# Block attention in four PSUM banks, its steps between the blocks of the first two gate projections; values feature-major

## What is computed

```python
qa, ka, va, qb, kb, vb, ga, gb = split(h @ w_in)      # 8 query heads of 128; ka, va have 2 heads; ga, gb are 2048 wide
ya = global_gqa(rope(rms(qa)), rope(rms(ka)), va)     # full softmax over 256 keys, 8 heads
yb = neighbourhood_attention(qb, kb, vb, nat_rpb)     # softmax over a window, with a bias, 8 heads
merged = sigmoid(ga) * (ya @ w_oa) + sigmoid(gb) * (yb @ w_ob)
x = x + g1 * (merged @ w_out)
# g1 and five more rows of 2048 come from c_act @ w_ada + b_ada
```

## Time and profile before

| | |
|---|---|
| time, median of 3 runs | 2335.82 us (2332.87 to 2339.69) |
| span of the profiled execution | 2332.2 us; its own time is not listed apart, the lowest of the three is 0.7 us above this span |
| PE busy, share of the span | 2252.8 us, 97% |
| DVE, ACT, POOL busy | 1497.0, 1010.8, 242.6 us |
| chain that ended last | PE 78%, DMA 9%, DVE 6%, issue 3%, ACT 2% |
| TensorE clock, mean over the span | 0.981 of full |

### The profile page before, as it was taken

The page is one execution under the profiler, slowest core; times in us unless marked ns, Lnnn a source line. Parts: engine busy times, 40 slices in busy tenths (PEclk is TensorE's granted clock), DMA queues, the critical chain, the costliest instruction groups (busy, mean ns, idle before and its releaser), DMA issues.

```text
span 2332.2 us, 38185 instructions
## 1 busy us (share of the span) xinstructions
PE 2252.8 (97%) x13068; PEld 1982.8 (85%) x13068; DVE 1497.0 (64%) x1990; ACT 1010.8 (43%) x1248; POOL 242.6 (10%) x425
## 2 busy tenths in 40 slices
PE   8999997999999989999999999999999999999997
PEld 6888686988877768899777878879999999998885
DVE  5666577897777857688677777774445444544544
ACT  5444534444444434434644443444434343443432
POOL 1110011212210021101022221210000000000000
PEclk9999998999999997999999999989999999999998
DMA  8786076887885583867359887755555655566563
GB/s 304 250 244 178 22 244 248 254 268 270 304 275 176 174 244 101 263 187 252 109 193 314 311 306 254 262 191 180 181 183 177 189 180 183 179 207 195 187 199 120
DMA packets 196653, 499.07 MB, mean 214 GB/s; under 512 B 29784, under 2 KB 56536, under 8 KB 195648
## 3 DMA queue, kind: packets, MB, share of 16 engines
q1 hardware_dynamic: 163648, 388.03, 51.3%
q0 software_dynamic: 32896, 109.55, 14.1%
HBM read 495.34 MB, written 2.10 MB: 213 GB/s over the span
## 4 chain that ended last, share of the span: by engine, by line
PE 78%; DMA 9%; DVE 6%; issue 3%; ACT 2%; POOL 1%; POOLq 0%; SPq 0%; DVEq 0%; ACTq 0%
PE ps L1678 39%; PE ps L1687 32%; DMA ada_raw<-in_w_ada_dram 6%; PE ps L1747 2%; DVE lo L926 1%; PE ps L1768 1%; PE ps L1838 1%; DVE acc_g L938 1%; DVE acc_s L938 1%; DMA raw<-in_w_in_dram 1%; PE ps L1757 1%; DMA raw<-in_ml_w_in_dram 1%; ACT hi L544 1%; DMA rel<-in_rpbT_dram 1%; DMA xT_raw<-in_xT_dram 0%
## 5 line engine op out<-in xcount | busy, mean ns | idle before, releaser
L926 DVE TENSOR_TENSOR lo<-raw,hi 128x1024 fp32r<-128x1024 f32 x732 | 891.4, 1223 | 631.7 <-ACT hi L544 629.6
L544 ACT CAST hi<-raw 128x1024 fp32r<-128x1024 f32 x732 | 767.8, 1051 | 1144.5 <-PE ps L1678 552.0
L1687 PE MATMUL ps<-XH,hi 128*128 (+1 forms) x1920 | 543.6, 283 | 1.9 <-DVE XL L1042 1.9
L1687 PE MATMUL ps<-XH,lo 128*128 (+1 forms) x1920 | 543.4, 283 | 0.0
L1687 PE MATMUL ps<-XL,hi 128*128 (+1 forms) x1920 | 543.4, 283 | 0.0
L1678 PE MATMUL ps<-hi,XH 128*128 128x512 f32 x1376 | 433.2, 394 | 34.2 <-DVE lo L926 28.4
L1678 PE MATMUL ps<-lo,XH 128*128 128x512 f32 x1376 | 428.9, 391 | 0.0
L1678 PE MATMUL ps<-hi,XL 128*128 128x512 f32 x1376 | 428.0, 390 | 0.0
L1687 PEld LDWEIGHTS ps<-XH,hi 128*128 128x128 f32 x1920 | 368.6, 192 | 2.5 <-DVE XL L1042 2.4
L1687 PEld LDWEIGHTS ps<-XL,hi 128*128 128x128 f32 x1920 | 368.6, 192 | 0.0
L1687 PEld LDWEIGHTS ps<-XH,lo 128*128 128x128 f32 x1920 | 368.6, 192 | 0.0
(11 more groups left out here) (309 smaller groups left out, 1645.6 us busy)
## 6 DMA issues: line engine op xcount, KB each, us to landing
ada_raw<-in_w_ada_dram POOLq DMA_DIRECT2D x384, 256.0 KB, 5.0
raw<-in_w_in_dram SPq DMA_DIRECT2D x136, 512.0 KB, 4.6
raw<-in_ml_w_in_dram SPq DMA_DIRECT2D x128, 512.0 KB, 5.1
raw<-in_w_gate_dram SPq DMA_DIRECT2D x176, 256.0 KB, 2.8
raw<-in_w_up_dram SPq DMA_DIRECT2D x176, 256.0 KB, 3.0
raw<-in_w_down_dram SPq DMA_DIRECT2D x88, 512.0 KB, 4.2
raw<-in_mla_w_in_dram SPq DMA_DIRECT2D x48, 512.0 KB, 5.6
raw<-in_mla_w_out_dram SPq DMA_DIRECT2D x32, 512.0 KB, 4.7
```

The lines of the kernel that those rows point to most:

```text
L544: nc.scalar.copy(hi[:, j, :], raw[:, j, :]).then_inc(hi_ready, 1)
L926: nc.vector.tensor_tensor(lo[:, j, :], raw[:, j, :], hi[:, j, :].bitcast(F32), ALU.subtract) \
L1687: ins = mm(ps[:, o:o + SEQ], w[:, j, m * P:(m + 1) * P], x(k), start=first and lead and m % 2 == 0, stop=last and w is lo, skip_group_chec ...
```

## The change

The block attention no longer stands ahead of the gate projections. It uses banks 4 to 7 only: two for scores, one (`turn_slot`) for the transposed probabilities of a head, one (`value_slot`) for its result. `ga0`, `ga1` and `gb0` all use group 0 (banks 0 to 3). A table `STEPS_AFTER` puts the steps 0 to 35 behind the blocks 0 to 30 counted from the start of `ga0`: one step behind each, two behind blocks 3, 6, 9, 12 and 15. On PE a step stands behind block b; on ACT and DVE the same step stands ahead of `hi` and `lo` of block b+4. Heads of `yb` now come first. DVE scales the probabilities instead of the result. The values are the stationary operand, and the result of a head comes out feature-major (two matmuls 128x256 per head), so the transposes back are gone. ACT copies the transposed probabilities once per head (128x512). The sigmoids of `ga0` and `ga1` are written where `vb_tok`, `kva_tok` and `kaT` lie, so they wait for heads of the attention. `ADA_BESIDE` moves ten ada blocks away from `ga0`.

```diff
-    "ga0@0:act ga1:act gb0:act gb1:act oa0:dve ob0:dve oa1:dve ob1:dve mTa:split4 wo0:dve mTb:split4 wo1@0:dve "
+    "ga0@0:act ga1@0:act gb0@0:act gb1:act oa0:dve ob0:dve oa1:dve ob1:dve mTa:split4 wo0:dve mTb:split4 wo1@0:dve "
...
-              "qa": 16, "kb": 8, "vb": 16, "ga0": 22, "ga1": 22, "gb0": 22, "gb1": 22, "oa0": 6, "ob0": 6, "oa1": 6,
-              "ob1": 6, "wo0": 20, "wo1": 20}
+              "qa": 18, "kva": 4, "kb": 8, "vb": 16, "ga0": 12, "ga1": 22, "gb0": 22, "gb1": 22, "oa0": 6, "ob0": 6,
+              "oa1": 6, "ob1": 6, "wo0": 22, "wo1": 22}
...
+STEPS_AFTER = {}
+_step = 0
+for _block in range(31):
+    _n = 2 if _block in (3, 6, 9, 12, 15) else 1
+    STEPS_AFTER[_block] = tuple(range(_step, _step + _n))
+    _step += _n
...
+        def score_slot(u):
+            return (4 + u % 2) * HALF
+        turn_slot, value_slot = 6 * HALF, 7 * HALF
...
@@ scalar @@
-            attention(A3, 32, prob2, probT2, nmax2, rsum2, lambda u: SEQ,
-                      lambda h: yaH[:, h, :] if h < N_A else ybH[:, h - N_A, :])
+            def blk_step(i):
+                if i < 32:
+                    act.wait_ge(A3["maxed"], i + 1)
+                    if i >= 3:
+                        act.wait_ge(A3["turned"], i - 2)
+                    o = score_slot(i)
+                    nc.scalar.activation(prob2[:, i % 3, :], ps[:, o:o + SEQ], ACT.Exp, bias=nmax2[:, i:i + 1],
+                                         accum_out=rsum2[:, i:i + 1]).then_inc(A3["exped"], 1)
+                if i >= 3 and i % 2 and i < 34:
+                    h = (i - 3) // 2
+                    act.wait_ge(A3["turned"], 2 * h + 2)
+                    if h:
+                        act.wait_ge(A3["summed"], h)
+                    nc.scalar.copy(probT2[:, :, :].rearrange(flat), ps[:, turn_slot:turn_slot + HALF]) \
+                      .then_inc(A3["copied"], 1)
+                if i >= 4 and i % 2 == 0:
+                    h = (i - 4) // 2
+                    H, _, hh = blk_head(h)
+                    act.wait_ge(A3["summed"], h + 1)
+                    nc.scalar.copy(H[:, hh, :], ps[:, value_slot:value_slot + SEQ]).then_inc(A3["hi"], 1)
...
+            for b in range(4, 48):
+                if b == 19:
+                    act.wait_ge(A3["summed"], N_A)
+                    gate("ga0", sig_a, 0)
+                if b == 35:
+                    act.wait_ge(A3["summed"], 2 * N_A)
+                    gate("ga1", sig_a, 1)
+                for i in STEPS_AFTER.get(b - 4, ()):
+                    blk_step(i)
+                hi_block(B_MERGE + b, b % RING, landed(B_MERGE + b, b % RING))
@@ vector @@
+            def blk_step(i):
+                if i < 32:
+                    o = score_slot(i)
+                    dve.wait_ge(A3["scored"], i + 1)
+                    add_bias(i, o)
+                    nc.vector.tensor_reduce(nmax2[:, i:i + 1], ps[:, o:o + SEQ], AX_X, ALU.max, negate=True) \
+                      .then_inc(A3["maxed"], 1)
+                if 1 <= i <= 32:
+                    u = i - 1
+                    dve.wait_ge(A3["exped"], u + 1)
+                    link(nc.vector.reciprocal(rinv2[:, u:u + 1], rsum2[:, u:u + 1]))
+                    nc.vector.tensor_scalar(prob2[:, u % 3, :], prob2[:, u % 3, :], rinv2[:, u:u + 1], None,
+                                            ALU.mult).then_inc(A3["normed"], 1)
+                if i >= 5 and i % 2:
+                    h = (i - 5) // 2
+                    H, L, hh = blk_head(h)
+                    dve.wait_ge(A3["hi"], h + 1)
+                    nc.vector.tensor_tensor(L[:, hh, :], ps[:, value_slot:value_slot + SEQ],
+                                            H[:, hh, :].bitcast(F32), ALU.subtract).then_inc(A3["lo"], 1)
@@ tensor @@
+            def blk_step(i):
+                if i < 32:
+                    h, t = (i % 16) // 2, slice(i % 2 * P, (i % 2 + 1) * P)
...
+                    if i >= 2:
+                        pe.wait_ge(A3["exped"], i - 1)
+                    o = score_slot(i)
+                    mm(ps[:, o:o + SEQ], q, k, start=True, stop=True, skip_group_check=True).then_inc(A3["scored"], 1)
+                if i >= 4 and i % 2 == 0:
+                    h = (i - 4) // 2
+                    pe.wait_ge(A3["copied"], h + 1)
+                    if h >= 1:
+                        pe.wait_ge(A3["lo"], h)
...
+                        ins = mm(ps[:, o:o + SEQ], v, probT2[:, t, :], start=(t == 0), stop=(t == TOK - 1),
+                                 skip_group_check=True)
+                    ins.then_inc(A3["summed"], 1)
+                if 2 <= i < 34:
+                    u = i - 2
+                    pe.wait_ge(A3["normed"], u + 1)
+                    if u >= 2 and u % 2 == 0:
+                        pe.wait_ge(A3["copied"], u // 2)
+                    for t in range(TOK):
+                        o = turn_slot + t * SEQ + u % 2 * P
+                        ins = nc.tensor.transpose(ps[:, o:o + P], prob2[:, u % 3, t * P:(t + 1) * P], ident[:, :])
+                    ins.then_inc(A3["turned"], 1)
...
+            for n, name in enumerate(("ga0", "ga1", "gb0")):
+                token_major(name, B_MERGE + 16 * n, 16, XH, XL, then=blk_after(16 * n))
             pe.wait_ge(A3["lo"], 16)
-            for n, name in enumerate(("ga0", "ga1", "gb0", "gb1")):
-                token_major(name, B_MERGE + 16 * n, 16, XH, XL)
+            token_major("gb1", B_MERGE + 48, 16, XH, XL)
```

More of the change, by code:

```diff
@@ L828, in _ @@
             whole("kaT", kaT[:, :, :].rearrange(flat), width=2 * SEQ)
-            attention(A3, 32, prob2, probT2, nmax2, rsum2, lambda u: SEQ,
-                      lambda h: yaH[:, h, :] if h < N_A else ybH[:, h - N_A, :])
-            fourth(B_MERGE)
-            rest(B_MERGE, 16)
-            for n, (name, sig) in enumerate((("ga0", sig_a), ("ga1", sig_a), ("gb0", sig_b), ("gb1", sig_b))):
-                first4(B_MERGE + 16 * (n + 1))
-                c0 = n % 2 * COLS
-                each_tok(name, lambda t: sig[:, t, c0:c0 + COLS], ACT.Sigmoid)
-                rest(B_MERGE + 16 * (n + 1), 16 if n < 3 else 8)
+            def blk_step(i):
[18 more added lines that the diff above has]
+                    nc.scalar.copy(H[:, hh, :], ps[:, value_slot:value_slot + SEQ]).then_inc(A3["hi"], 1)
@@ new lines, in gate @@
+            def gate(name, sig, q):
+                each_tok(name, lambda t: sig[:, q, t, :], ACT.Sigmoid)
+            fourth(B_MERGE)
+            for b in range(4, 48):
[8 more added lines that the diff above has]
+                hi_block(B_MERGE + b, b % RING, landed(B_MERGE + b, b % RING))
@@ L838, in _ @@
+            for n, (name, q) in enumerate((("gb0", 0), ("gb1", 1))):
+                first4(B_MERGE + 16 * (n + 3))
+                gate(name, sig_b, q)
+                rest(B_MERGE + 16 * (n + 3), 16 if n < 1 else 8)
             for n in range(3):
@@ L1511, in add_bias, with blk_before, do @@
                                                  ALU.add))
-            attention(A3, 32, nmax2, rsum2, rinv2, y_tok2, lambda u: SEQ, add_bias, None,
-                      lambda h: yaH[:, h, :] if h < N_A else ybH[:, h - N_A, :],
-                      lambda h: yaL[:, h, :] if h < N_A else ybL[:, h - N_A, :])
+            def blk_step(i):
[17 more added lines that the diff above has]
+                                            H[:, hh, :].bitcast(F32), ALU.subtract).then_inc(A3["lo"], 1)
+            def blk_before(off):
+                def do(b):
+                    for i in STEPS_AFTER.get(off + b - 4, ()):
+                        blk_step(i)
+                return do
             lo_block(B_MERGE + 3, 3)
-            rest(B_MERGE, 16, "ga0")
+            rest_blocks(B_MERGE, 4, 16, 16, "ga0", before=blk_before(0))
             for n, name in enumerate(("ga1", "gb0", "gb1")):
-                first4(B_MERGE + 16 * (n + 1))
-                rest(B_MERGE + 16 * (n + 1), 16, name)
+                n0, before = B_MERGE + 16 * (n + 1), blk_before(16 * (n + 1))
+                for b in range(RING):
+                    before(b)
+                    lo_block(n0 + b, b)
+                rest_blocks(n0, 4, 16, 16, name, before=before)
             first4(B_MERGE + 64)
@@ L1951, in _, with blk_after, do @@
+            def blk_after(off):
+                def do(b):
+                    for i in STEPS_AFTER.get(off + b, ()):
+                        blk_step(i)
+                return do
+            for n, name in enumerate(("ga0", "ga1", "gb0")):
+                token_major(name, B_MERGE + 16 * n, 16, XH, XL, then=blk_after(16 * n))
             pe.wait_ge(A3["lo"], 16)
[L1952 to L1953 removed]
+            token_major("gb1", B_MERGE + 48, 16, XH, XL)
```

67 lines of the change are left out of this document (33 added, 34 removed).

## The result

The changed kernel takes 2373.89 us (median of 4 executions, 2363.66 to 2384.68) where the kernel before, timed beside it, takes 2337.76 (2332.87 to 2341.08): a ratio of 1.0154, 95% interval 1.0133 to 1.0175. It is slower by 36 us; 2366 was predicted, range 2345 to 2379 (one of the four executions, 2384.68, lies above that range).

What follows compares the result with a forecast made beforehand. PE bounds the kernel before; after the change, a ring of ACT and DVE waits would pace it. PE work 210.4, waits 37.7, late `lo` 3.0 and half clock 8 make 259.1 against 229.2 us: 2335.8 + 30 = 2366, range 2345 to 2379.

Steps and rivals of the forecast that it cites:

- PE's own work, at full clock: First score to `oa0`: 64 blocks of 2.72 us (174.1) plus 32 attention units of 1.08 us (34.6).
- waits, blocks 4 to 12: PE waits 4.3 us in each of three three-block cycles with bias and one ada block per block: 12.9 us.
- read-out of `ga0`: Behind block 15: PE waits 4.8 us for table loads, sigmoids, exponential and copy, since all gate blocks share group 0.
- waits, blocks 16 to 27: Turns without bias, with 22 ada blocks, take 4.96 us: 13.9 us of PE waits, less 2.9 of DVE lead, 11.0.
- late `lo` in `gb0`, `gb1`: PE waits for `lo` blocks held up behind ada DMAs: half of the earlier 6.0 us kept, 3.0 us.
- half clock: 1.7 us at the stretch's start, plus six waits of 3.5 us or longer costing 1.7 each, 8 of 10.2 counted.
- The ring: Bias, maximum, exponential, copy or rounding, `hi`, `lo`, ada block, next bias: 5.01 us per turn against PE's 3.80.
- The table load: At the read-outs, 1.30 us from load to next instruction, by the trace, not the skill page's 2.66 with drain.
- the first case: The ring turns and the clock is lost at the long waits: 2359 to 2371 us; chance 0.45.
- the third: Every 2 us wait in blocks 16 to 27 also brings half clock, and table-load drains cost extra: 2377 us; chance 0.16.
- The one that waits at the read-outs and four times inside pairs: The ring isn't closed, PE stays the bound; only read-outs and copies within pairs wait: stretch 230.2, 2337 us; chance 0.07.
- The one with the pairs' copies in time: PE stays the bound, ACT and DVE run ahead within three blocks of `lo` stock: stretch 221.7, 2328 us; chance 0.10.

Runs made afterwards that it cites:

- e1: Changed kernel, with `hi` of a block ahead of the attention steps on ACT: 2347.07 us, ratio 1.0030 to the kernel before.
- e5: Changed kernel, with DVE doing the ada blocks ahead of `lo` in `ga0` and `ga1`: 2355.46 us, ratio 1.0091 to the kernel before.
- e9: Changed kernel with the old ada counts (ten more ada blocks in `ga0`): 2375.06 us, ratio 1.0156 to the kernel before.
- e10: e8 with the ada blocks ahead of `lo` in `ga0` and `ga1`: 2333.26 us, ratio 0.9969 to the kernel before.
- e11: e8 with four ada blocks moved from `wo0` and `wo1` back to `ga0`: 2327.57 us, ratio 0.9950 to the kernel before.
- e2: Changed kernel, with pairs of steps behind blocks 4, 7, 10, 13, 16, one block later: 2356.57 us, ratio 1.0071 to the kernel before.
- e6: Changed kernel, with `hi` ahead of the steps and pairs one block later: 2334.90 us, ratio 0.9993 to the kernel before.
- e7: Changed kernel, with ACT's wait for the heads one block earlier, so the sigmoid table loads early: 2368.01 us, ratio 1.0134 to the kernel before.
- e3: Kernel before, with the changed kernel's new ada counts only: 2340.23 us, ratio 1.0005 to the kernel before.
- e12: Kernel before, with four ada blocks moved from `ga0` to `wo0` and `wo1`: 2339.47 us, ratio 1.0004 to the kernel before.
- e8: Changed kernel, with `hi` ahead of the steps, pairs behind blocks 4, 7, 10, 13, 28, table load early: 2329.25 us, ratio 0.9968 to the kernel before.

## Why the prediction was right, and where its terms were off

The direction and the cause hold, and so does the size: +30 us predicted, +36 measured. That the stretch came out at 259.8 us with 259.1 predicted is luck: the waits and the late `lo` were put 10.2 us too high, PE's work and the clock 10.9 us too low, and the two cancel.

| term | predicted | measured |
|---|---|---|
| PE's own work, at full clock | 208.7 | 212.2 |
| waits, blocks 0 to 3 | 5.5 | 4.9 (4.15, 0.7) |
| waits, blocks 4 to 12 | 12.9 | 10.6 (3.52, 3.52, 3.53) |
| waits, blocks 13 to 15 | 0 | 0 |
| read-out of `ga0` | 4.8 | 4.6 |
| waits, blocks 16 to 27 | 11.0 | 7.0 (1.71, 1.84, 1.18, 2.27) |
| read-out of `ga1` | 3.5 | 3.4 |
| late `lo` in `gb0`, `gb1` | 3.0 | 0 |
| half clock | 1.7 + 8 | 17.1 |
| sum | 259.1 | 259.8 |

- **The ring** is shown by taking out one member at a time: `hi` (e1, -26 us), the ada block (e5, -22), ten more ada blocks put in (e9, +7.5), and by the same edit doing nothing once the ring is open (e10). Bias to bias took 4.95 us in a turn with a copy (1158.94 to 1163.89) and 4.71 in the next, with a rounding (to 1168.60), predicted 5.01 on average. In `ga0` every wait stood where it was put: the values' matmul of every third block, and the two read-outs.
- **PE's own work** was 3.5 us too small. PE was busy for 229.3 us of the stretch; less 17.1 for the clock, that is 212.2. From score to score, two blocks and two steps took 7.68 us (1158.32 to 1166.00), 3.84 each instead of 3.80; that is 1.3 of the 3.5, the rest wasn't found. e10 and e11, whose stretches have no half clock at all, agree: PE is busy for 212.1 us in each.
- **The waits** were too large by 7.2. The long waits of `ga0` ended at 1152.81, 1170.76, 1189.88 and 1207.92 us, 18.0, 19.1 and 18.0 apart, predicted 16.8. The turn with the pair is what was mis-sized: bias to bias 8.3 to 9.5 us (9.45 from 1168.60 to 1178.05), not 6.8, by the leg through PE's values and by a wait of 0.8 to 1.9 us for the next score. It makes the cycle longer but PE's wait no longer, since PE is working, at half clock, in that time. In blocks 16 to 27 (11.0, 7.0 measured) the turn was right, 4.84 us on average over nine (maximum to maximum, 1240.11 to 1283.70), predicted 4.96; but PE first waits at 1254.6. The 6.8 us of half clock behind the read-out of `ga0`, in which PE falls back by some 3 us without waiting, would account for most of that; no run tests it. The 3.0 for late `lo` didn't appear in this profile: in `gb0` and `gb1` DVE still waits 12.8 us for ada DMAs, but PE doesn't wait for `lo`. In the profiles of e1, e2, e5, e6, e7 and e9 it does, for 0.5 to 2.4 us, so the term wasn't without ground.
- **The clock** is the term with the worst size: 9.7 against 17.1. A wait was priced at 3.4 us of half clock because both rows of before showed that. Four of seven took twice as long. The 17.1 is half of 37.6 less 3.3 us in which PE was idle at the low clock (such as 1169.8 to 1170.76). The page that I cited (the Trainium skill, TensorE: Matmul & The Clock Gate, HAM oscillation) says of a loop that waits in each turn that the slow clock is paid again each time; at the six waits of 3.4 us and more the trace of the changed kernel agrees. Its waits of 1.2 to 1.8 us in blocks 16 to 27 brought no half clock.
- **The table load** costs 1.30 us to the next instruction at all three loads (1222.68 to 1223.98, 1225.93 to 1227.23, 1300.40 to 1301.69; the second begins 0.01 us after the sigmoids end, so nothing lies hidden ahead of it), not the 2.66 of the Trainium skill's page (ScalarE: Activation LUTs, "What ACT_TABLE_LOAD costs"); going by the row was right. e7 shows that it was on the path.
- **Outside the stretch** the time grew by 7.5 us: 1.1 ahead of it, which is less than single executions differ there (1131 to 1141 us over all profiles, whose ada counts in `qa` and `kva` differ in part), and 6.4 behind it. The moved ada blocks had been priced at nothing, at most 3. By the traces they cost more than that behind `oa0` (more waits, and 20.4 us of half clock between 1515 and 1640 us, against 13.6 before); by the timed runs of e3 and e12 some 3 or less.
- **The rivals.** The measured 2373.9 lies between the first case (2359 to 2371) and the third (2377), but not for the third's reasons: of the four waits in blocks 16 to 27 only the one of 2.27 us brought half clock, and no drain shows behind the loads. What the first case lacked is the second 3.4 us of half clock at four of the waits. The two in which PE stays the bound are near what the kernel becomes once `hi` stands ahead of the steps. The one that waits at the read-outs and four times inside pairs had 230.2 us; e1 waits there and nowhere else for long, and took 233.7, 5.7 of it half clock's cost where the rival had 1.7. The one with the pairs' copies in time had 221.7; e6, with the pairs moved too, took 221.5. Both failed for the changed kernel because its turns take 4.7 us and more, not under 3.8.

## What to carry to other kernels

When steps of one job are put between blocks of another, write down for each engine what its next instruction waits for, follow that from queue to queue until it closes, and compare the time of one round with what the bounding engine has to do meanwhile; the order within a block (which of two independent instructions a queue gets first) decided here between +1.5% and +0.3% by itself (e1), and together with the place of the pairs, of the table load and of the ada blocks between +1.5% and -0.3 to -0.5% (e8, e11). Put the operand that the bounding engine needs soonest from each queue first, and the filler (here the ada blocks) where that queue waits anyway. An edit's worth depends on whether its instruction is in the ring at present: here one edit gave 22 us or nothing.
